# Down products and scatter of each expert body, moved one body later

## What is computed

```python
for g in range(N_GROUPS):
    hg = silu(einsum('nd,edf->nef', xn, w_gate[g])) * einsum('nd,edf->nef', xn, w_up[g])
    y = y + einsum('nef,efd->nd', hg * combine[:, g, :, None], w_down[g])
return h + y
```

## Time and profile before

| what | value |
|---|---|
| median of 3 runs | 671.71 us (671.52 to 671.83) |
| profiled execution, its span | 669.8 us |
| PE, DVE, ACT, POOL busy | 650.2, 390.7, 215.9, 101.4 us |
| first body starts, last down product ends | 409.4, 658.3 us |
| weight loads of the experts | 96 DMAs of 1024 KB |

### The profile page before, as it was taken

The page is one execution under the profiler, slowest core; times in us unless marked ns, Lnnn a source line. Parts: engine busy times, 40 slices in busy tenths (PEclk is TensorE's granted clock), DMA queues, the critical chain, the costliest instruction groups (busy, mean ns, idle before and its releaser), DMA issues.

```text
span 669.8 us, 10196 instructions
## 1 busy us (share of the span) xinstructions
PE 650.2 (97%) x3969; PEld 466.9 (70%) x3969; DVE 390.7 (58%) x736; ACT 215.9 (32%) x448; POOL 101.4 (15%) x138
## 2 busy tenths in 40 slices
PE   5799999999999999999989999999999999999998
PEld 3579999988888888888779995354544445453535
DVE  4648335678897878785674667453443535251615
ACT  6346232234534444422435565302020201110112
POOL 3300015899300000000000010110110101010010
PEclk9899999999999999999999999999999999999999
DMA  7432223202232121112345057999999999999943
GB/s 242 147 125 65 64 65 97 92 1 64 79 100 74 60 68 52 68 44 90 126 166 243 33 219 284 381 408 412 401 422 397 423 394 420 407 418 404 417 185 126
DMA packets 49794, 138.72 MB, mean 207 GB/s; under 512 B 6202, under 2 KB 28235, under 8 KB 41556
## 3 DMA queue, kind: packets, MB, share of 16 engines
q1 hardware_dynamic: 47298, 134.37, 52.8%
q0 software_dynamic: 2304, 3.64, 1.5%
q10 hardware_dynamic: 146, 0.07, 0.0%
HBM read 138.62 MB, written 4.19 MB: 213 GB/s over the span
## 4 chain that ended last, share of the span: by engine, by line
PE 87%; DVE 6%; ACT 3%; issue 2%; DMA 1%; POOL 0%; ACTq 0%; DVEq 0%
PE bank L990 16%; PE bank L608 12%; PE bank L609 12%; PE bank L610 12%; PE bank L1004 8%; PE bank L1114 8%; PE bank L850 1%; DVE y_lo L1903 1%; PE bank L1015 1%; PE bank L877 1%; PE bank L874 1%; ACT whi L1233 1%; DVE sig_a L1617 1%; DVE sig_a L1613 1%; DMA wraw<-in_w_out 1%
## 5 line engine op out<-in xcount | busy, mean ns | idle before, releaser
L990 PE MATMUL bank<-w_pair,xgT 128*64 128x512 f32 x512 | 113.8, 596 | 0.0
L990 PEld LDWEIGHTS bank<-w_pair,xgT 128*64 128x64 f32 x512 | 35.2, 137 | 66.4 <-issue 65.4
L1547 DVE TENSOR_TENSOR wlo<-wraw,whi 128x2048 fp32r<-128x2048 f32 (+1 forms) x25 | 56.4, 2258 | 20.3 <-ACT whi L1233 20.3
L608 PE MATMUL bank<-whi,xhi 128*128 128x256 f32 x224 | 64.4, 288 | 0.0
L609 PE MATMUL bank<-wlo,xhi 128*128 128x256 f32 x224 | 63.0, 281 | 0.0
L610 PE MATMUL bank<-whi,xlo 128*128 128x256 f32 x224 | 62.9, 281 | 0.0
L608 PE MATMUL bank<-xhi,whi 128*128 128x512 f32 x152 | 61.4, 404 | 0.0
L609 PE MATMUL bank<-xlo,whi 128*128 128x512 f32 x152 | 60.1, 396 | 0.0
L610 PE MATMUL bank<-xhi,wlo 128*128 128x512 f32 x152 | 59.7, 393 | 0.0
L1004 PE MATMUL bank<-w_pair,hT 128*64 128x512 f32 x256 | 58.1, 595 | 0.0
L1880 DVE SCALAR_TENSOR_TENSOR hg<-bank,pair_w,hs 128x256 f32<-128x256 f32 x16 | 7.7, 483 | 80.6 <-ACT hs L1452 80.6
(11 more groups left out here) (331 smaller groups left out, 1330.9 us busy)
## 6 DMA issues: line engine op xcount, KB each, us to landing
w_pair<-in_expert_w_gate SPq DMA_DIRECT2D x32, 1024.0 KB
w_pair<-in_expert_w_up SPq DMA_DIRECT2D x32, 1024.0 KB
w_pair<-in_expert_w_down SPq DMA_DIRECT2D x32, 1024.0 KB, 17.4
wraw<-in_w_in SPq DMA_DIRECT2D x17, 1024.0 KB, 5.6
wraw<-in_w_out SPq DMA_DIRECT2D x4, 1024.0 KB, 5.3
h<-in_x SPq DMA_DIRECT2D x4, 512.0 KB, 5.3
wraw<-in_w_gla_branch SPq DMA_DIRECT2D x2, 1024.0 KB, 5.0
wraw<-in_w_attn_branch SPq DMA_DIRECT2D x2, 1024.0 KB, 5.2
```

The lines of the kernel that those rows point to most:

```text
L608: nc.tensor.matmul(ps, lhi(k), rhi(k), start=(k == 0), stop=False)
L990: last = nc.tensor.matmul(tiles[GU_BANK[s]][j * SLOT:(j + 1) * SLOT, :].rearrange("p (f n) -> p f n", f=2), xgT[:, k, s * P + j * SLOT:s * ...
L1547: nc.vector.tensor_tensor(wl, raw, wh.bitcast(F32), ALU.subtract).then_inc(s_lo, 1)
```

## The change

From body 2 on, down and scatter on TensorE belong to the body before. The order of a body i from 2 to 6 becomes: gate/up of both pairs, down of body i - 1 (all 64 columns wide), then hidden transposes of both pairs, row transposes for body i + 1, scatter of body i - 1, slot products and one-hot transposes for body i + 2 (all 128 columns). Body 0 keeps its own down and scatter, behind its gate/up; body 1 has neither; body 7 does those of body 6, and then its own, and the last scatter. ScalarE's `y_hi` and VectorE's `y_lo` and adds move along. SyncE issues a down load after down of the body before, so one body later than now. The banks are dealt anew: hidden in bank 5 (a down bank, so the hidden transposes wait for `y_lo` of the first pair), slot products in 2, one-hots in 3; `onehot` has two buffers. Work and number of products stay the same.

```diff
         assert len(consts) == CONST_DMAS

         first_flipped = [tiles[FIRST_FLIP_BANK][:, s * 2 * P:(s + 1) * 2 * P].bitcast(BF16) for s in range(2)]
-        flipped = [tiles[k][:, 0:2 * P].bitcast(BF16) for k in OH_BANK]
+        flipped = [tiles[OH_BANK][:, s * 2 * P:(s + 1) * 2 * P].bitcast(BF16) for s in range(2)]
+
+        def slots(j, s):
+
+            c = 32 * (j % 2) + 16 * s
+            return tiles[W_BANK][:, c:c + 8]
+
+        def hidden_bank(s):
+            return tiles[H_BANK][:, s * 2 * P:(s + 1) * 2 * P]

         block = ctx.enter_context(nc.Block())
...
@@ -1036,76 +1044,31 @@
                         pe.wait_ge(s_add[k], r * (2 * BODIES) + 1)
                     for s in range(2):
                         pe.wait_ge(s_idx[s], r * BODIES + 1)
+                    slot_values(1)
+                    for s in range(2):
                         last = slot_matmul(s, 0, 2, 8)
                     last.then_inc(s_pwm, 1)

-                for i in range(BODIES):
-                    n = r * BODIES + i
-
-                    pe.wait_ge(s_xgT[0], n + 1)
-                    pe.wait_ge(s_wgu[0], 64 * n + 64)
-                    expert_gate_up(i, 0, 0)
-                    if i == 0:
-                        first_slot_weights()
-                    pe.wait_ge(s_xgT[1], n + 1)
-                    expert_gate_up(i, 0, 1).then_inc(s_gu[0], 1)
-                    if i == 0:
-                        pe.wait_ge(s_pw, n + 1)
-                        slot_values(1)
-                        for s in range(2):
-                            pe.wait_ge(s_ohT[s], n + 1)
-                        onehot_transposes()
-                    pe.wait_ge(s_xgT[2], n + 1)
-                    pe.wait_ge(s_wgu[1], 64 * n + 64)
-                    expert_gate_up(i, 1, 0)
-                    pe.wait_ge(s_xgT[3], n + 1)
+                def down(i, n):
+
                     for k in range(4):
                         pe.wait_ge(s_add[k], 2 * n + 1)
-                    if i == 0:
-                        pe.wait_ge(s_pw, n + 2)
-                    if i + 2 < BODIES:
-                        slot_values(i + 2)
-                    elif i + 1 == BODIES:
-                        for s in range(2):
-                            pe.wait_ge(s_oh[s], n + 2)
-                            slot_matmul(s, 0, 0, 2).then_inc(s_tkm[s], 1)
-                    pe.wait_ge(s_hg[0], n + 1)
-                    hidden_transposes(0)
-                    if i == 0:
-                        for s in range(2):
-                            pe.wait_ge(s_ohT[s], r * BODIES + 2)
-                    if i + 2 != BODIES:
-                        onehot_transposes()
-                    expert_gate_up(i, 1, 1).then_inc(s_gu[1], 1)
-
-                    if i + 2 < BODIES:
-                        pe.wait_ge(s_pw, n + 3)
-                        for s in range(2):
-                            pe.wait_ge(s_ohT[s], r * BODIES + i + 3)
-                    elif i + 1 == BODIES:
-                        for s in range(2):
-                            pe.wait_ge(s_idx[s], n + 2)
-                            pe.wait_ge(s_ohT[s], n + 2)
-                    pe.wait_ge(s_hT[0], n + 1)
-                    pe.wait_ge(s_wd[0], 32 * n + 32)
-                    expert_down(0, 0)
-                    pe.wait_ge(s_hg[1], n + 1)
-                    hidden_transposes(1)
-                    expert_down(0, 1).then_inc(s_down[0], 1)
-                    pe.wait_ge(s_hT[1], n + 1)
-                    pe.wait_ge(s_wd[1], 32 * n + 32)
-                    expert_down(1, 0)
-                    expert_down(1, 1).then_inc(s_down[1], 1)
-
-                    if i + 1 == BODIES:
-                        last_scatter(i, n)
-                        row_transposes(i + 1)
-                        continue
-                    row_transposes(i + 1)
+                    for s in range(2):
+                        pe.wait_ge(s_hT[s], n + 1)
+                    for s in range(2):
+                        pe.wait_ge(s_wd[s], 32 * n + 32)
+                        expert_down(s, 0)
+                        expert_down(s, 1).then_inc(s_down[s], 1)
+
+                def scatter(i, n):
+
                     for s in range(2):
                         pe.wait_ge(s_ylo[s], n + 1)
                     for u in range(8):
                         b, half = u // 2, u % 2
+                        if u == 2 and i >= 1:
+                            for s in range(2):
+                                pe.wait_ge(s_hT[s], n + 2)
                         if u >= 4:
                             pe.wait_ge(s_add[u % 4], 2 * n + 2)
                         cols_ = slice(half * 512, (half + 1) * 512)
@@ -1115,6 +1078,67 @@
                                                         part[s][:, cols_], start=(s == 0 and part is y_hi),
                                                         stop=(s == 1 and part is y_lo))
                         last.then_inc(s_sc[u % 4], 1)
+
+                for i in range(BODIES):
+                    n = r * BODIES + i
+
+                    pe.wait_ge(s_xgT[0], n + 1)
+                    pe.wait_ge(s_wgu[0], 64 * n + 64)
+                    expert_gate_up(i, 0, 0)
+                    pe.wait_ge(s_xgT[1], n + 1)
+                    expert_gate_up(i, 0, 1).then_inc(s_gu[0], 1)
+                    if i == 0:
+                        first_slot_weights()
+                        for s in range(2):
+                            pe.wait_ge(s_ohT[s], n + 1)
+                        onehot_transposes(1)
+                    pe.wait_ge(s_xgT[2], n + 1)
+                    pe.wait_ge(s_xgT[3], n + 1)
+                    pe.wait_ge(s_wgu[1], 64 * n + 64)
+                    expert_gate_up(i, 1, 0)
+                    expert_gate_up(i, 1, 1).then_inc(s_gu[1], 1)
+                    if i >= 2:
+                        down(i - 1, n - 1)
+                        pe.wait_ge(s_ylo[0], n)
+                    elif i == 1:
+                        pe.wait_ge(s_add[2], 2 * n + 1)
+
+                    for s in range(2):
+                        pe.wait_ge(s_hg[s], n + 1)
+                        hidden_transposes(s)
+                    if i == 0:
+                        pe.wait_ge(s_pw, n + 2)
+                        slot_values(2)
+                        for s in range(2):
+                            pe.wait_ge(s_ohT[s], n + 2)
+                        onehot_transposes(2)
+                        down(0, n)
+                    if i + 1 < BODIES:
+                        ahead = 2 if i == 0 else 1
+                        pe.wait_ge(s_pw, n + ahead + 1)
+                        for s in range(2):
+                            pe.wait_ge(s_ohT[s], n + ahead + 1)
+                        row_transposes(i + 1)
+                    if i == 0:
+                        scatter(0, n)
+                    elif i >= 2:
+                        scatter(i - 1, n - 1)
+                    if i >= 1 and i + 2 < BODIES:
+                        pe.wait_ge(s_xgT[3], n + 2)
+                        slot_values(i + 2)
+                        pe.wait_ge(s_xgT[2], n + 2)
+                        onehot_transposes(i + 2)
+                    elif i + 1 == BODIES:
+                        for s in range(2):
+                            pe.wait_ge(s_oh[s], n + 2)
+                            slot_matmul(s, 0, 0, 2).then_inc(s_tkm[s], 1)
+                        onehot_transposes(0)
+                        down(i, n)
+                        for s in range(2):
+                            pe.wait_ge(s_idx[s], n + 2)
+                            pe.wait_ge(s_ohT[s], n + 2)
+                        last_scatter(i, n)
+                        row_transposes(i + 1)

         @block.sync
...
@@ -1145,14 +1169,27 @@
                             src.rearrange("o (k p) n -> p (o k) n", p=P)
                         sp.dma_start(we[s][j][i][:, :, :], src).then_inc((s_wgu if gate_up else s_wd)[s], 16)

-            def reload(i, n):
+            def next_gate_up(i, n):

                 for s in range(2):
                     sp.wait_ge(s_gu[s], n)
                     load(2 * i + s, s, True)
+
+            def next_down(i, n):
+
                 for s in range(2):
                     sp.wait_ge(s_down[s], n)
                     load(2 * i + s, s, False)
+
+            def bodies_after_first(n):
+
+                next_gate_up(1, n + 1)
+                next_down(1, n + 1)
+                next_gate_up(2, n + 2)
+                with sp.Fori(2, BODIES - 1) as i:
+                    next_gate_up(i + 1, n + i + 1)
+                    next_down(i, n + i)
+                next_down(BODIES - 1, n + BODIES - 1)

             sp.wait_ge(s_mlo, KT)
             load(0, 0, True)
@@ -1170,14 +1207,14 @@
             sp.wait_ge(s_cast, 2)
             load(0, 0, False, (1,))
             load(1, 1, False)
-            with sp.Fori(1, BODIES) as i:
-                reload(i, i)
+            bodies_after_first(0)
```

(119 more changed lines are left out.)

49 lines of the change are left out of this document (22 added, 27 removed).

## The result

The changed kernel takes 676.8 us in the median (675.2 to 678.5), the kernel before, timed beside it, 671.8; the ratio is 1.0074 (95% interval 1.0053 to 1.0094). The prediction was 673.5 us with a range of 670.4 to 676.0: the sign was right, the size was too small by 3.3 us. The profiled execution has a span of 676.6 us, 6.8 us over that of before. It is the slowest of four: two others took 675.2 and 675.8 us with a mean granted clock of 0.995, and the profiled one 678.5 us with 0.990.

What follows compares the result with a forecast made beforehand. PE was taken as the bound, with the DMA queue just behind. PE ready at 469.2 plus 197.5 gives 666.7 us; the 4.8 us weight wait makes 671.5, and 1.9 to the median 673.5; range 670.4 to 676.0.

Steps and rivals of the forecast that it cites:

- What bounds the kernel now: Whole span: PE is the bound, busy for 97%, with the DMA queue close behind at 410 to 412 GB/s.
- Part 1, fewer runs: 64-column runs on PE fall from 26 to 11; each costs 0.30 us, so a full body loses 0.6 us.
- Part 2, the y wait: Wait before scatter: of 0.42 us about 0.05 stay; full body 31.1 us, one without slot products 30.4.
- Part 3, the seams: Bodies 0, 1 and 7: waits left open there; body 0 33.8 us, body 1 19.0, body 7 about 38.
- Part 4, the weights of body 2: Second gate/up pair of body 2: weights complete at 474.0, PE ready at 469.2, a wait of 4.8 us.
- My own check on the kernel before: The queue count applied to the kernel before: last landing of a body put at 453.7, measured 455.0, 1.3 us more.
- part 5: From body 2's second pair to the end of the span: 197.5 us, with no later wait for weights.
- (a): Second pair of body 2: PE waits 4 to 6 us; time 672.6 to 674.8 us; chance 0.5.
- (b): Same place: wait only 2 to 3.9 us, queue at 420 GB/s; time 671.0 to 672.5 us; chance 0.27.
- (c): Same place: weights there at or soon after 469.2, so faster, 668.7 to 670.3 us; chance 0.08.
- (d): Body 2's down or later gate/up: queue binds again, or y chain stays open; 675 to 676.5 us; chance 0.1.
- The 358 GB/s: The skill's HBM limit to one core; by it the end would be 8 us later still; given no weight.

Runs made afterwards that it cites:

- the last experiment: The kernel before without the two down DMAs of the second pair in each body from 1 on: 671.7 us, ratio 0.9997.
- the repaired kernels: Changed kernel with down of body 1 at the end of body 1's row transposes, 671.7 us; the same with three more edits, 670.8 us.
- the filler kernel: The changed kernel with filler products in TensorE's idle stretches around the late weights of body 2: 675.7 us, ratio 1.005.

## Why the prediction was off, step by step

- **What bounds the kernel now**: right. PE alone, shown by the last experiment.
- **Part 1, fewer runs**: right. 0.33 us a cut against 0.30.
- **Part 2, the y wait**: right. Full bodies 31.03 to 31.06 us against 31.1, body 6 30.37 against 30.4.
- **Part 3, the seams**: right in the sum. Body 0 34.1 us against 33.8, body 1 19.2 against 19.0, body 7 to the end of its down products 38.6 against 38.2, where the wait for the last adds is 0.5 us and was put at 0.1. Not in the sum: the first pair of body 2 waited 0.9 us for its weights and then ran 1.8 us longer at the low clock. Neither shows in the end, since the second pair was later still.
- **Part 4, the weights of body 2**: the place and the kind were right, the size was short. PE started the second pair at 475.9, not at 474.0, and later than the latest end that I gave (474.8). 0.4 us of the 1.9 is a later start of the stage. Most of the rest lies in the loads of body 1: by my count their last landing is at 419.5 + 30.4 + 2.4 = 452.3, and it came at 453.9, 1.6 us later. My own check on the kernel before had shown 1.3 us of this kind, of which I took in 0.5. The eight loads behind it took 21.9 us against 21.4. The path from the freed buffer, 24.9 us, was not in the working. The wait itself is 3.2 us, less than the 4.8 forecast, only because the first pair ended late; without that it would be about 5 (an estimate: 475.9 - 463.95 - 7.02).
- **Missing altogether**: the clock. The sum priced a wait as its own length. The products behind it ran at 1.2 GHz for 6 us and gave away 3.1 us. This is the step that failed. Add it: the second pair at 475.9, its 3.1 us, and the 197.5 us of part 5 give 676.5, measured 676.6. With the late landing alone the forecast would have been 675.4 in the median, inside the range. This sum is for the profiled execution. The median is 3.3 us above the forecast and not 5.0, and the traces with the same kind of wait lost 1.9 us twice, and 2.9 and 3.1 us once each, so the clock's part differs from execution to execution. The Trainium skill (TensorE: Matmul & The Clock Gate, HAM oscillation) says it: a wait for a transfer between products lets the clock fall, and the next products start at the low rate. The trace agrees (0.50 in 476 to 478), and the filler kernel, with the same traffic and the second pair in 7.09 us, shows the cause.
- **Part 5**: right, 197.6 us without the clock's part against 197.5; no later body waited.
- **The rivals**: (a) held in kind, with a later landing and a larger price. (b) and (c) needed faster loads than came. (d), a queue that binds again, did not happen in the changed kernel, where body 2's long wait let the queue catch up; it is what the repaired kernels met (31.5 to 32.1 us a body).
- **The 358 GB/s** got no weight, rightly: 415 GB/s over whole bodies.

## What to carry to other kernels

A software pipeline moves work away from one body, and this body's time is what hid the next loads: compare the shortened body with the time from a freed buffer to the last landing (here 19 us against 25) before you count the gain of the others. Price a wait of TensorE as its length plus what the products behind it lose at half clock (here 1.9 to 3.1 us), and put work that is ready into it rather than leave it idle. When PE's side and the queue's side are as close as here (31.05 and 31.6 us a body), look for the holes in the queue first: here the order of two loads decided about 0.25%.

## What I had not expected of the hardware

- Behind the wait in body 2 TensorE ran at a granted clock of 0.50 for about 6 us of dense products. In the kernel without the second pair's loads 1.8 us were lost behind idle stretches of at most 1.6 us; of the six traces that have these stretches, three show this fall.
- Leaving out 4 MB of loads ahead moved a landing by nothing: eight DMAs of 1024 KB took 24.8 us from issue to last landing into an empty queue, and 24.9 us behind a full one. Without gathers beside them it was 23.5.
- PE's products were not slowed by the weight traffic: 32.06 us a body at 345 GB/s and 32.04 at 410, and 32 records in 7.09 us beside 426 GB/s.
